# Grouped attention heads: six of the eight query pairs come from DRAM as 32x32 blocks and are turned on VectorE instead of TensorE

## Time and profile before

| | |
|---|---|
| median of 3 runs | 1035.84 us (1035.31 to 1036.29) |
| the profiled execution | 1036.18 us |
| its span, first to last instruction | 1034.4 us |
| busy over the span: PE, DVE, ACT, POOL | 97%, 82%, 74%, 47% |
| mean granted TensorE clock | 0.992 |

### The profile page before, as it was taken

One profiled execution on the slowest core, in us unless ns is written; L12 is line 12 of the kernel. 1 busy time (PEld: TensorE's weight loads), 2 busy tenths in 40 slices (PEclk: granted clock), 3 DMA queues, 4 the chain that ended last, 5 costly groups with the idle time before them and its releaser, 6 DMA issues.

```text
span 1034.4 us, 15653 instructions
## 1 busy us (share of the span) xinstructions
PE 1005.1 (97%) x5055; PEld 806.5 (78%) x5055; DVE 851.3 (82%) x1064; ACT 760.3 (74%) x1022; POOL 483.4 (47%) x423
## 2 busy tenths in 40 slices
PE   8999999999999999995999999999999999999997
PEld 7999986666656688874888888888888888888885
DVE  6788778887888533378999999999999999999982
ACT  7665658888989745547787887778877888788772
POOL 2477679634687655427443244324442344324011
PEclk9999999999999999997999999999999999999999
DMA  9344240432343398854999999999999999999982
GB/s 329 68 123 130 82 161 11 129 66 64 123 128 72 125 252 239 233 147 147 394 393 403 398 408 410 402 400 397 420 401 401 398 419 400 402 397 410 412 337 41
DMA packets 109133, 276.02 MB, mean 267 GB/s; under 512 B 58321, under 2 KB 66732, under 8 KB 85404
## 3 DMA queue, kind: packets, MB, share of 16 engines
q1 hardware_dynamic: 103280, 258.11, 67.3%
q0 software_dynamic: 5744, 17.29, 6.7%
q10 hardware_dynamic: 60, 0.01, 0.0%
HBM read 247.46 MB, written 27.92 MB: 266 GB/s over the span
## 4 chain that ended last, share of the span: by engine, by line
PE 51%; DMA 1%; DVE 1%; issue 0%; ACT 0%; POOLq 0%; POOL 0%
PE ps L2213 11%; PE ps L2215 11%; PE ps L2214 11%; PE ps L2229 5%; PE ps L2227 5%; PE ps L2228 5%; PE ps L2180 1%; DMA out<-y,give 1%; DMA xt<-h,idxT 0%; DVE idx L1965 0%; DVE affT L1974 0%; DVE gates L1960 0%; POOLq L2487 0%; POOL out L2172 0%; ACT y L2341 0%
## 5 line engine op out<-in xcount | busy, mean ns | idle before, releaser
L2383 DVE TENSOR_TENSOR lo<-raw,hi 128x2048 fp32r<-128x2048 f32 x191 | 430.6, 2285 | 29.6 <-ACT hi L2305 29.4
L2305 ACT ACTIVATE hi<-raw 128x2048 fp32r<-128x2048 f32 x192 | 364.2, 1917 | 67.4 <-PE ps L2215 56.6
L2213 PE MATMUL ps<-hi,xehi 128*128 128x512 f32 x480 | 188.4, 393 | 0.1
L2215 PE MATMUL ps<-hi,xelo 128*128 128x512 f32 x480 | 187.1, 390 | 0.0
L2214 PE MATMUL ps<-lo,xehi 128*128 128x512 f32 x480 | 186.7, 389 | 0.0
L2137 POOL DMA_INDIRECT xe<-h,take x60 | 110.7, 1845 | 25.1 <-issue 13.7
L2132 POOL COPY take<-idx 128x4 uint32 (+1 forms) x15 | 31.0, 2067 | 188.6 <-DVE xt L2399 188.3
L1471 DVE TENSOR_REDUCE nmax<-ps 128x1 f32<-128x512 f32 x128 | 85.9, 681 | 28.3 <-PE ps L1300 15.1
L2215 PEld LDWEIGHTS ps<-hi,xelo 128*128 128x128 f32 x480 | 90.1, 188 | 19.1
L2213 PEld LDWEIGHTS ps<-hi,xehi 128*128 128x128 f32 x480 | 90.3, 188 | 18.6 <-issue 0.5
L2214 PEld LDWEIGHTS ps<-lo,xehi 128*128 128x128 f32 x480 | 90.2, 188 | 18.3
(11 more groups left out here) (311 smaller groups left out, 2061.2 us busy)
## 6 DMA issues: line engine op xcount, KB each, us to landing
raw<-in_w_down SPq DMA_DIRECT2D x64, 1024.0 KB, 10.3
raw<-in_w_gate SPq DMA_DIRECT2D x60, 1024.0 KB, 10.5
raw<-in_w_up SPq DMA_DIRECT2D x60, 1024.0 KB, 10.0
w_raw<-in_w_in SPq DMA_DIRECT2D x8, 592.0 KB, 8.4
x<-in_x SPq DMA_DIRECT2D x8, 512.0 KB, 5.3
r<-reciprocal_sums SPq DMA_DIRECT2D x32, 128.0 KB, 3.0
attention_out<-pj SPq DMA_DIRECT2D x16, 256.0 KB, 2.3
woraw<-in_w_o SPq DMA_DIRECT2D x4, 1024.0 KB, 6.1
```

The costliest lines, as they stand in the source:

```text
L2213: pe.matmul(ps[:, dst[n], :], rowhi[:, c, :], hi[w][:, cols], start=c == 0, stop=False)
L2215: last = pe.matmul(ps[:, dst[n], :], rowlo[:, c, :], hi[w][:, cols], start=False, stop=c == KD - 1)
L2305: act.activation(hi[s][:], raw[r][:], ACT.Copy).then_inc(hi_done, 1)
L2383: dve.tensor_tensor(lo[s][:], raw[r][:], hi[s][:].bitcast(F32), ALU.subtract).then_inc(lo_done, 1)
```

## The change

The queries of pairs 4 and 6 of the first set and of all four pairs of the second are no longer turned by PE. SP loads a pair's 128 columns as four DMAs of 32x32 squares into `qb`, from `pj_dram` for the first set and from a new array `pq_dram` for the second; DVE turns them in one instruction of 128 partitions into `qT`; ACT and DVE make the two heads' high and low parts from there. Pairs 0 and 2 stay as they were. The items (6 pairs and 16 latent heads) share the two buffers in the order of their use, so the rounds in which SP loads them move: the first two loads of the program are now pairs 4 and 6, and heads 8 and 9 are loaded in rounds 1 and 2. The store of round 1 takes the second set's grouped queries too: eight DMAs, four of 256 KB and four of 384 KB.

```diff
+    pq_dram = nc.dram_tensor("second_pq", [P, TS, C_K], F32).ap()
...
-    latent_query = lambda kind, g: kind == "q" and g % HEADS >= QH
-    transposed = [sum(1 for p in preps[:n + 1] if not second(*p) and not latent_query(*p)) for n in range(len(preps))]
-    latent_heads = [g for g in range(ALL) if latent_query("q", g)]
+    by_blocks = lambda kind, g: kind == "q" and g >= GROUP
+    transposed = [sum(1 for p in preps[:n + 1] if not second(*p) and not by_blocks(*p)) for n in range(len(preps))]
+    block_items = [p for p in preps if by_blocks(*p) and not second(*p)]
+    item_of = {p: block_items.index((p[0], p[1] - second(*p))) for p in preps if by_blocks(*p)}
+    users = [[prep_index[p] for p in preps if item_of.get(p) == m] for m in range(len(block_items))]
+    squares = lambda kind, g: QK // SQUARE if kind == "q" and g % HEADS >= QH else P // SQUARE
+    blocks_in = [sum(squares(*p) for p in block_items[m % 2:m + 1:2]) for m in range(len(block_items))]
...
+    loads_in = {1: ((2,), ()), 2: ((3,), ()), 3: ((4, 5), ()), 4: ((6, 7), ()), 5: ((8, 9), ()), 6: ((10, 11), ()),
+                7: ((12,), ()), 8: ((13,), ()), 9: ((14,), ()), 10: ((15,), ()), 11: ((16, 17), ()), 12: ((18, 19), ()),
+                13: ((20, 21), ())}
...
-        def store_queries():
+        def store_rows():
+            pj, q_rows, kv_rows = att["rows"][1]
+            sp.wait_ge(rows_ready, T)
             for i in range(TS):
-                sp.dma_start(q_dram[1, :, i, :], att["rows"][1][1][:, i].rearrange("p h c -> p (h c)")).then_inc(q_stored, 16)
-
-        def load_queries(g):
-            m = latent_heads.index(g)
+                sp.dma_start(pq_dram[:, i, :], pj[:, i, 0:C_K]).then_inc(q_stored, 16)
+                sp.dma_start(q_dram[1, :, i, :], q_rows[:, i].rearrange("p h c -> p (h c)")).then_inc(q_stored, 16)
+
+        def load_blocks(m):
+            kind, g = block_items[m]
+            h, first = g % HEADS, g < HEADS
             if m >= 2:
                 sp.wait_ge(q_turned, m - 1)
-            if m == MH:
-                sp.wait_ge(q_stored, W_LOADED + 16 * TS)
-            for a in range(QK // SQUARE):
-                c = (g % HEADS - QH) * QK + a * SQUARE
-                sp.dma_start(qb[m % 2][a * SQUARE:(a + 1) * SQUARE],
-                             q_dram[g // HEADS, :, :, c:c + SQUARE].rearrange("(b s) i r -> s i b r", s=SQUARE)).then_inc(qb_loaded[m % 2], 16)
+            if not first and block_items[m - 1][1] < HEADS:
+                sp.wait_ge(q_stored, W_LOADED + 16 * 2 * TS)
+            if h < QH:
+                rows, at = pj_dram if first else pq_dram, h * HD
+            else:
+                rows, at = q_dram[g // HEADS], (h - QH) * QK
+            for b in range(squares(kind, g)):
+                c = at + b * SQUARE
+                sp.dma_start(qb[m % 2][b * SQUARE:(b + 1) * SQUARE],
+                             rows[:, :, c:c + SQUARE].rearrange("(b s) i r -> s i b r", s=SQUARE)).then_inc(qb_loaded[m % 2], 16)
...
-        load_queries(QH)
-        load_queries(QH + 1)
+        load_blocks(0)
+        load_blocks(1)
         for n in range(HEAD_PAIRS):
-            first = HEADS + QH if n == HEADS // 2 - 2 else 2 * n + 4
-            if first % HEADS > QH or n == HEADS // 2 - 2:
-                load_queries(first)
-                load_queries(first + 1)
+            for m in loads_in.get(n, ((), ()))[0]:
+                load_blocks(m)
...
             if n == 1:
-                store_queries()
+                store_rows()
...
-            if second(kind, g) or latent_query(kind, g):
+            if second(kind, g) or by_blocks(kind, g):
                 return
...
-            if latent_query(kind, g):
-                act.wait_ge(q_turned, latent_heads.index(g) + 1)
+            if by_blocks(kind, g):
+                act.wait_ge(q_turned, item_of[kind, g] + 1)
...
-            src = qT if latent_query(kind, g) else ps[:, PREP, :]
+            src = qT if by_blocks(kind, g) else ps[:, PREP, :]
...
-        def turn_queries(g):
-            m = latent_heads.index(g)
-            dve.wait_ge(qb_loaded[m % 2], W_LOADED + 16 * (QK // SQUARE) * (m // 2 + 1))
+        def turn_blocks(m):
+            rows = squares(*block_items[m]) * SQUARE
+            dve.wait_ge(qb_loaded[m % 2], W_LOADED + 16 * blocks_in[m])
             if m:
-                dve.wait_ge(prep_lo, prep_index["q", latent_heads[m - 1]] + 1)
-            dve.transpose(qT[0:QK, :], qb[m % 2][0:QK].rearrange("p i b r -> p (i b r)")).then_inc(q_turned, 1)
-
-        turn_at = {u - 1: g for u, listed in due.items() for kind, g in listed if latent_query(kind, g)}
+                dve.wait_ge(prep_lo, users[m - 1][-1] + 1)
+            dve.transpose(qT[0:rows, :], qb[m % 2][0:rows].rearrange("p i b r -> p (i b r)")).then_inc(q_turned, 1)
+
+        turn_at = {u - 1: item_of[p] for u, listed in due.items() for p in listed if p in block_items}
...
             if u in turn_at:
-                turn_queries(turn_at[u])
+                turn_blocks(turn_at[u])
```

More of the change, by code:

```diff
@@ L330, in build @@
         project_and_attend(nc, a, x_dram, k, temps, w, att, wo, pj, q_rows, kv_rows, w_raw, uq_raw, ukv_raw,
-                           ps, banks, o_dram, r_dram, wo_loaded, pj_dram, q_dram, kv_dram,
+                           ps, banks, o_dram, r_dram, wo_loaded, pj_dram, q_dram, kv_dram, pq_dram,
                            moe, out_rows, h2_rows, raw_loaded, out, h2_dram)
@@ L1010, in project, with attend @@
     return (sync_program, gpsimd_program, tensor_program, scalar_program, vector_program), signals
-def attend(phase, project_signals, a, k, att, wo, ps, banks, o_dram, r_dram, q_dram, wo_loaded):
+def attend(phase, project_signals, a, k, att, wo, ps, banks, o_dram, r_dram, pj_dram, q_dram, kv_dram, pq_dram, wo_loaded):
     rows_ready, mla_ready, kv_done, proj_done, row_copied, pj_back, mla_back, xlo_done, clo_done, ones_ready = (
@@ L1073, in attend @@
     qb, qT = att["qb"], att["qT"]
+    loads_in = {1: ((2,), ()), 2: ((3,), ()), 3: ((4, 5), ()), 4: ((6, 7), ()), 5: ((8, 9), ()), 6: ((10, 11), ()),
+                7: ((12,), ()), 8: ((13,), ()), 9: ((14,), ()), 10: ((15,), ()), 11: ((16, 17), ()), 12: ((18, 19), ()),
+                13: ((20, 21), ())}
+    assert [m for n in sorted(loads_in) for part in loads_in[n] for m in part] == list(range(2, len(block_items)))
     def rows_of(g):
@@ L1158, in sync_program @@
             spread_reciprocals(n)
+            for m in loads_in.get(n, ((), ()))[1]:
+                load_blocks(m)
             if n == 1:
-                store_queries()
+                store_rows()
             if n == HEADS // 2 + 1:
@@ L2477, in project_and_attend @@
 def project_and_attend(nc, a, x_dram, k, temps, w, att, wo, pj, q_rows, kv_rows, w_raw, uq_raw, ukv_raw,
-                       ps, banks, o_dram, r_dram, wo_loaded, pj_dram, q_dram, kv_dram, moe, out_rows, h2_rows, raw_loaded, out, h2_dram):
+                       ps, banks, o_dram, r_dram, wo_loaded, pj_dram, q_dram, kv_dram, pq_dram, moe, out_rows, h2_rows, raw_loaded, out, h2_dram):
     with Phase(nc, "p") as phase:
@@ L2482, in project_and_attend @@
                                             ps, banks, pj_dram, q_dram, kv_dram)
-        attend_programs, attend_signals = attend(phase, signals, a, k, att, wo, ps, banks, o_dram, r_dram, q_dram, wo_loaded)
+        attend_programs, attend_signals = attend(phase, signals, a, k, att, wo, ps, banks, o_dram, r_dram, pj_dram, q_dram, kv_dram, pq_dram,
+                                                  wo_loaded)
         (route_sync, route_gpsimd, route_tensor, route_scalar, route_vector), route_signals = route(
```

## The result

| | before | after |
|---|---|---|
| median of 18 runs each | 1036.26 us (1035.31 to 1036.74) | 1038.14 us (1037.20 to 1039.71) |
| ratio, 95% interval | | 1.0020 (1.0013 to 1.0026) |
| profiled execution, its span | 1036.18, 1034.4 | 1039.71, 1037.9 |

The change makes the kernel slower, by 1.9 us in the medians. The execution that was profiled is the slowest of the 18, so its losses are read for their places first and for their sizes second. It is 3.53 us longer than the profiled one before: 2.86 in the loop and 1.29 behind the last matmul (see under e8), less 0.62 elsewhere.

What follows compares the result with a forecast made beforehand. PE was taken as nearly gapless in the two grouped stages, with ACT and DVE having 15 to 20% left. Gain 1.73 less 0.2 (second reader) and 0.2 (SP's queue) is 1.3 us: median 1034.5 us, range 1032.9 to 1037.0.

Steps and rivals of the forecast that it cites:

- What the pairs give: Six pairs in the grouped stages: of PE's 2.84 us at most, 1.73 us stay as gain.
- the bound in head 22: At pair 22 ACT also scales output weights, busy 24.50 of 26 us, so only 0.1 us is gained.
- The step that failed: SP's queue, second set: output weights come 2.7 us later, waited for by nothing tight, so no cost was put down.
- what is won in the loop reaches the end: Attention loop to output projection: PE is busy 30.00 of 30.00 us there, with nothing in between running to its own date.
- VectorE's second reader: Grouped low parts now have two SBUF inputs, so GpSimd holds DVE; nearly all covered by DVE idling: 0.2 us lost.
- Head 9's blocks behind the eight stores: SP's queue: head 9's blocks land on time by 0.1 us; 0.2 us put down as loads may land later.
- Late blocks for head 9: Rival, behind the eight stores: blocks come late, giving back 0.66 us, for 1035.0 us; chance 0.19.
- VectorE held by GpSimd, on the path: Rival, at the 12 low parts of the grouped stages: price 4.7 us in place of 0.2, 1039.0 us; chance 0.13.
- PE's price in full: Rival, in every pair's slot: PE is the bound and all 2.84 us are won, 1033.0 us; chance 0.20.
- What would make the prediction wrong: Sign: PE waits for ACT or DVE in the slots of the pairs, or the stages gain over 2 us.

Runs made afterwards that it cites:

- e8: Changed kernel with output weights first, head 9's blocks ahead of the eight stores, head 26's blocks earlier, and all turns into PSUM: 1033.82 us.
- e11: Changed kernel with grouped turns into PSUM, output weights ahead of pair 22's blocks, head 26's blocks a round earlier: 1035.08 us.
- e10: Kernel before, without the change, but block loads of heads 24 and 25 put ahead of the output weights: 1038.31 us.
- e6: Changed kernel with only the turns of the six grouped pairs going into an unused PSUM bank: 1037.98 us.
- e1: Changed kernel with the first two output weight loads issued ahead of pair 22's blocks: 1037.14 us.
- e2: Changed kernel with head 9's blocks loaded behind those of head 8, ahead of the eight stores: 1038.10 us.
- e3: Changed kernel with DVE turning all blocks, grouped and latent, into an unused PSUM bank: 1035.42 us.
- e7: Changed kernel with only SP's queue reordered: output weights first, head 9's blocks ahead of the eight stores, head 26's blocks earlier: 1035.57 us.

## Why the prediction was wrong

**What the pairs give: right.** The sum said 1.73 us. By the slots of e11 it is 2.0: pair 6 0.42 (forecast 0.36), pair 16 0.40 (0.41), pair 18 0.45 (0.36), pair 20 0.40 (0.2), pair 22 0.31 (0.1), pair 4 nothing (0.3). ACT was not the bound in head 22 as I took it to be. At pair 4 the loop is 0.43 us ahead at the end of head 3 and level at the end of head 4: the exponential behind the late query took it. The turn takes 0.70 us on 128 partitions, as assumed.

**The step that failed** is the sentence that the output weights come 2.7 us later, "waited for by nothing tight, so nothing is put down". They came 4.0 us later (2.65 for the blocks ahead; the rest because the store of heads before these stood at 262.02 in place of 260.70), and the slack was 2.3 us: the second half was issued at 261.66, took 8.7 us to land, and ACT scales at 272.64. I named the delay and did not look up who waits for the weights and when. In the trace it cost 2.57 us, and by e10 such a delay costs 1.8 us by itself, the size of the whole loss. The premise that what is won in the loop reaches the end, with nothing that runs "to its own date", failed as well: inside the loop the weights do, and the blocks of head 26. What the pairs win before head 20 comes back as waiting there, as e6 shows.

**VectorE's second reader: seen, mis-sized, and half of it missed.** The term was 0.2 us, with DVE as the one that is held. Its long low parts are there (913 ns median, up to 1823), and mostly hidden as argued; one, at head 22, is on the path and costs 0.65 us by itself. The other direction was not in the sum: GpSimd is held by DVE, and GpSimd, busy 43.6 of 47.6 us, has no slack in the first set. Its three holds, of 0.29, 0.35 and 0.32 us, put head 7 0.92 us behind (after against e6). Head 9's blocks behind the eight stores had a term of 0.2. The trace has 0.70, but e6 and e1 have next to nothing there, the one without these holds and the other with them (-0.48 to -0.52 and +0.46 to +0.39 from head 7 to head 10); so the 0.70 isn't shown to be owed to GpSimd, nor to be there in most executions. The Trainium skill (SBUF — State Buffer, Who interferes with whom) says that the order of issue decides which of the two engines is blocked; the trace agrees, with 0.56 us for POOL's copy behind DVE and 0.21 without. I cited the rule and used only one of its two directions.

**The sum of the costs.** In medians, from the changed kernel (+1.88) to the change without its own costs (e11, -1.43) is 3.3 us. The two causes don't add up one by one: taking only the second reader out shows nothing in the median (e6), only the weights' order 1.0 us (e1), and in their traces each hands much of its gain to the next date in the queue.

**The rivals.** "Late blocks for head 9" happened in the profiled execution, at about the price given (0.66), and by e2 decides nothing alone. "VectorE held by GpSimd, on the path" got the sign right, but its 4.7 us were too much, and its place holds for head 22 alone; at head 7 it is GpSimd that is held, and the 2.57 us of head 20 are SP's. "PE's price in full" is what the loop comes to once the costs are out, but for pair 4. What would make the prediction wrong was named rightly: PE waits for ACT, 0.60 us at pair 4 and 1.77 in head 20.

## What to carry to other kernels

When a change puts issues into a queue that is written out by hand, list every load behind them in the same round with its issue, its landing and its first reader: a slack of 2.3 us against a delay of 4.0 was there to be read. Gains in a loop last only until the next load that runs to its own date, so a repair that shows nothing in its own total may still belong to the cause; test repairs together too, and look in the trace at what ended later. And if an operand moves from PSUM to SBUF on VectorE, look at what GpSimd does at that time and whether it has slack, not only at VectorE. Here a free PSUM bank as the target of the turn kept that from happening, and with the queue's order it made a kernel faster than both, 1033.57 us.

## What the hardware showed that was not expected

- A DVE instruction of 0.7 us with two SBUF inputs delays GpSimd by 0.29, 0.35 and 0.32 us in the three cases shown (0.90 against 0.61, 0.56 against 0.21, 1.06 against 0.74), and in the third DVE's own time is untouched (0.69).
- Where DVE was the one held, it ended 0.54 or 0.55 us after GpSimd's instruction in all eight cases of the changed kernel's trace that lasted over a microsecond. But as under L529 in the earlier trace rows, the low part at 169.31 took only 0.73 us inside a GpSimd instruction of 2.91 us (L530, from 169.28).
- A long wait of PE can cost more than itself. PE stood over 1.5 us at one time in three of the loops: 1.77 us here, 1.76 in e1 and 2.22 in e6. In e1 and e6 the granted clock fell to 0.50 for 3.4 us some 1.6 us after PE went on; here it stayed at 1.00.
- SP's stores are not evenly priced: in this trace 0.43 to 0.73 us each, but 1.25 for two of the eight, so that eight took 6.25 us where four had taken 2.82.
- ACT reads a turned query from PSUM in 0.59 us (e3) and from SBUF in 0.63, so the bank as a target costs ACT nothing.
- Executions of the variants lie further apart than those of the kernel before: 1034.57 to 1038.78 in e7, against 1035.52 to 1036.98. The clock's fall (e1, e6) and the wait behind the last matmul (e8) are two things that differ by over a microsecond between traces; that they make up the spread isn't shown.
